# A hybrid encoder step on one core: weight splits started one phase earlier, and attention scores as three rounded products

## What is computed

```python
xn = rmsnorm(x, norm1_w)
proj = xn @ w_in                      # z | x,B,C | dt | q | k | v
y_ssm = ssm_group(...)                # conv, chunked scan, gate, norm
o_sb  = stick_breaking(q, k, v, ...)  # z = q.k * 64**-0.5 ; suffix sums of log-sigmoid ; w @ v
h = x + concat(y_ssm, o_sb) @ w_out
...
def peer_rows(xr, wq, k1, k2, u_tab, v_tab):
    q = xr @ wq
    ...                               # top 16 per half, then top 16 of the sums
    act  = gelu(u_tab[expert] @ xr)
    coef = softmax(best) * act
    return sum(coef * v_tab[expert])
out = rmsnorm(h + peer(rmsnorm(h, norm2_w)))
```

## Time and profile before

| | us |
|---|---|
| median of 3 runs (3828.84 to 3840.70) | 3835.93 |
| the profiled execution | 3835.56 |
| its span in the profile | 3833.8 |
| PE busy in it | 3375.1 |
| DVE busy in it | 2605.1 |
| POOL busy in it | 1772.6 |
| ACT busy in it | 1103.4 |

### The profile page before, as it was taken

The page is one execution under the profiler, slowest core; times in us unless marked ns, Lnnn a source line. Parts: engine busy times, 40 slices in busy tenths (PEclk is TensorE's granted clock), DMA queues, the critical chain, the costliest instruction groups (busy, mean ns, idle before and its releaser), DMA issues. The chain is left out here.

```text
span 3833.8 us, 47422 instructions
## 1 busy us (share of the span) xinstructions
PE 3375.1 (88%) x16719; PEld 2866.7 (75%) x16719; DVE 2605.1 (68%) x4637; ACT 1103.4 (29%) x2170; POOL 1772.6 (46%) x1282
## 2 busy tenths in 40 slices
PE   5998799596899989999998689895999997888998
PEld 4998644333478989999998688884887775667776
DVE  3412644264536888999996466665887786988995
ACT  2322243232322211111111222222443333433343
POOL 1000143666300000688887578885888884333320
PEclk9999787686899999999999799997999998999999
DMA  2123099999611125555554699998999998999995
GB/s 78 49 78 126 18 419 371 324 316 324 215 68 60 38 70 170 170 178 167 175 174 130 236 333 354 346 344 304 353 363 345 347 345 310 407 388 400 401 386 181
DMA packets 281863, 945.35 MB, mean 247 GB/s; under 512 B 54432, under 2 KB 155936, under 8 KB 218688
## 3 DMA queue, kind: packets, MB, share of 16 engines
q1 hardware_dynamic: 209280, 583.52, 43.5%
q0 software_dynamic: 70656, 352.78, 24.1%
q10 hardware_dynamic: 1728, 6.49, 0.4%
HBM read 742.76 MB, written 199.45 MB: 246 GB/s over the span
## 5 line engine op out<-in xcount | busy, mean ns | idle before, releaser
L1579 POOL DMA_INDIRECT scratch_gates<-routes_merged,routes_at x768 | 1020.9, 1329 | 631.6 <-DVE routes_merged L1811 363.9
L2037 PE MATMUL val_acc<-n_hi 128*128 128x512 f32 x1536 | 617.3, 402 | 135.0 <-DVE n_lo L2072 132.1
L2038 PE MATMUL val_acc<-n_lo,n_hi 128*128 128x512 f32 x1536 | 609.5, 397 | 0.0
L2039 PE MATMUL val_acc<-n_hi,n_lo 128*128 128x512 f32 x1536 | 608.7, 396 | 0.0
L1626 POOL DMA_INDIRECT sparse_rows<-in_uv_rows,routes_at x256 | 382.4, 1494 | 379.3 <-DVE mixed L1660 322.1
L1637 DVE CUSTOM_DVE_ANT_0 sparse_rows<-sparse_rows,mixed 128x1024 f32<-128x1024 f32 x288 | 350.6, 1220 | 208.4 <-DMA sparse_rows<-in_uv_rows,routes_at 187.2
L2037 PEld LDWEIGHTS val_acc<-n_hi 128*128 128x128 f32 x1536 | 295.1, 192 | 225.5 <-DVE n_lo L2061 147.8
L123 PE MATMUL route_hidden<-n_hi,route_u_both 128*128 128x384 f32 x1280 | 432.5, 338 | 11.5 <-DMA route_u_both<-scratch_u_split 11.5
L124 PE MATMUL route_hidden<-n_lo,route_u_both 128*128 128x384 f32 x1280 | 434.3, 339 | 0.0
L125 PE MATMUL route_hidden<-n_hi,route_u_both 128*128 128x384 f32 x1280 | 432.8, 338 | 0.0
L1660 DVE SCALAR_TENSOR_TENSOR mixed<-sparse_rows,sparse_coef,mixed 128x1024 f32<-128x1024 f32 x288 | 363.7, 1280 | 9.4 <-ACT sparse_coef L1651 9.1
(11 more groups left out here) (288 smaller groups left out, 6225.1 us busy)
## 6 DMA issues: line engine op xcount, KB each, us to landing
val_v_raw<-in_v_rows SPq DMA_DIRECT2D x256, 512.0 KB, 6.9
scratch_u_split<-sb_u_both SPq DMA_DIRECT2D x80, 1024.0 KB, 5.1
route_u_both<-scratch_u_split SPq DMA_DIRECT2D x80, 1024.0 KB, 5.6
scratch_gates<-gate POOLq DMA_DIRECT2D x32, 1536.0 KB, 80.2
val_gate<-scratch_gates SPq DMA_DIRECT2D x256, 192.0 KB, 7.4
val_coef<-scratch_hidden SPq DMA_DIRECT2D x256, 192.0 KB, 7.8
conv<-in_peer_u SPq DMA_DIRECT2D x80, 512.0 KB, 6.0
scratch_hidden<-route_hidden_out SPq DMA_DIRECT2D x160, 192.0 KB
```

Of the source, the lines that this page charges most:

```text
L1579: pool.indirect_dma_start(self.t["gates"].rearrange("c r (l o) -> (c r l) o", o=1), bass.IndirectOffsetOnAxis(ap=self.routes.at[:, i, slot ...
L2037: nc.tensor.matmul(out, c_hi[:, s, tok], v_hi[:, s, to], start=(j == 0), stop=False)
L2038: nc.tensor.matmul(out, c_hi[:, s, tok], v_lo[:, s, to], start=False, stop=False)
L2039: last = nc.tensor.matmul(out, c_lo[:, s, tok], v_hi[:, s, to], start=False, stop=(j == KEYS - 1))
```

## The change

- 54 of the 80 ahead-of-time splits move from attention to the input projection. There POOL itself issues the loads and the stores, in the order load j+1, split j, store j; the landing place is part of `mixed`, which the first norm no longer needs. SP waits for the last stores ahead of the tails of the convolution. Attention keeps 26 splits, in buffers of its own.
- Attention's prompt scores become three products of fp32r parts with 64 rows. ACT writes `q_hi` (with the scale, in place of the scaling of q) and `k_hi`, DVE `q_lo` and `k_lo`, once for each pair.
- The inputs of pairs 2 and 3 are loaded behind the 26 splits, each as soon as its buffer is free.
- `conv` and `gate` are freed ahead of attention, which makes room for the new buffers.
- 320 scatters instead of 350 are issued in routing, and 460 instead of 500 by the end of the hidden phase, so 308 instead of 268 in the first value pass.

```diff
-SCATTER_FROM, ROUTE_SCATTERS = 17, 350
-HIDDEN_SCATTERS = 500
+SCATTER_FROM, ROUTE_SCATTERS = 17, 320
+HIDDEN_SCATTERS = 460
-PAIR_LOADS = {30: 2, 57: 3}
+FIRST_SPLITS = 54
...
+        presplit = Presplit(nc, t, sb, sem, raw, 0, FIRST_SPLITS)
...
                 with sp.Fori(1, pairs) as i:
                     load(i)
+                presplit.end(sp)
                 sp.wait_ge(convolved, STEPS * (CONV_TILES + 2))
...
                 nc.gpsimd.memset(result[:, :, :TAPS - 1], 0.0).then_inc(cleared, 1)
+                presplit.load(pool, 0)
+                for j in range(FIRST_SPLITS):
+                    if j + 1 < FIRST_SPLITS:
+                        presplit.load(pool, j + 1)
+                    presplit.split(pool, j)
+                    presplit.store(pool, j)
...
-                for j in range(EARLY_ROUTE):
-                    if j + 1 < EARLY_ROUTE:
+                for j in range(presplit.tiles):
+                    if j + 1 < presplit.tiles:
                         presplit.load(sp, j + 1)
                     presplit.store(sp, j)
-                    if j in PAIR_LOADS:
-                        p = PAIR_LOADS[j]
-                        sp.wait_ge(pv_done, 4 + JN * (p - 1))
-                        inputs.load(sp, p, p % 2)
+                for p in range(2, PAIRS):
+                    sp.wait_ge(pv_done, 4 + JN * (p - 1))
+                    inputs.load(sp, p, p % 2)
                 presplit.end(sp)
...
-                    nc.scalar.activation(q[:, u, :PROMPT], q[:, u, :PROMPT], ACT.Copy, scale=HD ** -0.5).then_inc(scaled, 1)
+                    nc.scalar.activation(q_hi[:, u], q[:, u, :PROMPT], ACT.Copy, scale=HD ** -0.5).then_inc(scaled, 1)
+                    nc.scalar.activation(k_hi[:, u], k[:, u, :PROMPT], ACT.Copy).then_inc(scaled, 1)
...
-                        last = nc.tensor.matmul(z[:, job.slot, job.cols], k[hp, u, job.j * P:job.j * P + P],
-                                                q[hp, u, job.qb * QW + job.lo:job.qb * QW + QW],
-                                                start=True, stop=True, skip_group_check=True)
+                        out = z[:, job.slot, job.cols]
+                        nc.tensor.matmul(out, k_hi[hp, u, keys], q_hi[hp, u, queries], start=True, stop=False, skip_group_check=True)
+                        nc.tensor.matmul(out, k_hi[hp, u, keys], q_lo[hp, u, queries], start=False, stop=False, skip_group_check=True)
+                        last = nc.tensor.matmul(out, k_lo[hp, u, keys], q_hi[hp, u, queries], start=False, stop=True, skip_group_check=True)
...
-                    pe.wait_ge(scaled, 3 * p + 3)
+                    pe.wait_ge(scaled, 4 * p + 4)
+                    pe.wait_ge(low_ready, 2 * p + 2)
...
+                    dve.wait_ge(scaled, 4 * p + 3)
+                    nc.vector.scalar_tensor_tensor(q_lo[:, u], q[:, u, :PROMPT], HD ** -0.5, q_hi[:, u].bitcast(F32),
+                                                   ALU.mult, ALU.subtract).then_inc(low_ready, 1)
+                    dve.wait_ge(scaled, 4 * p + 4)
+                    nc.vector.tensor_tensor(k_lo[:, u], k[:, u, :PROMPT], k_hi[:, u].bitcast(F32), ALU.subtract).then_inc(low_ready, 1)
```

More of the change, by code:

```diff
@@ L247, in spread, with input_projection @@
     return last
-def input_projection(nc, consts, x_hi, x_lo, dt_raw, conv_wb, conv, gate, t):
+def input_projection(nc, consts, x_hi, x_lo, dt_raw, conv_wb, conv, gate, t, raw):
     STEPS = TAPS + 1
@@ L806, in load, with attention_phase @@
                      t["past_v"][bass.ds(p, 1)].rearrange("a p b d -> (a p) (b d)")).then_inc(landed, 16)
-def attention_phase(nc, consts, t, inputs, mixed, zeros, raw, zeroed):
+def attention_phase(nc, consts, t, inputs, mixed, zeroed):
     jobs = attention_jobs()
@@ L825, in attention_phase @@
         strict, strict_masked, neg_ones = sb("strict", [P, P]), sb("strict_masked", [P, P]), sb("neg_ones", [P, P])
+        q_hi, q_lo = sb("q_hi", [P, 2, PROMPT], F32R), sb("q_lo", [P, 2, PROMPT], F32R)
+        k_hi, k_lo = sb("k_hi", [P, 2, PROMPT], F32R), sb("k_lo", [P, 2, PROMPT], F32R)
+        low_ready = sem("low_ready")
         z = ps("z", [P, 4, QW])
@@ L835, in attention_phase @@
             sem("sums_ready"), sem("w_ready"), sem("pv_done"), sem("o_copied"), sem("dve_step"), sem("passed"))
-        presplit = Presplit(nc, t, sb, sem, raw)
+        zeros = sb("zeros", [P, ZERO_COLS])
+        presplit = Presplit(nc, t, sb, sem, sb("u_raw", [P, 2, DC, P]), FIRST_SPLITS, EARLY_ROUTE - FIRST_SPLITS)
         def keys_of(job):
@@ L861, in _ @@
                 nc.gpsimd.memset(q_diag[:], 0.0).then_inc(cleared, 1)
-                nc.gpsimd.memset(zeros, 0.0).then_inc(zeros_cleared, 1)
+                nc.gpsimd.memset(zeros[:], 0.0).then_inc(zeros_cleared, 1)
                 pool.wait_ge(zeros_cleared, 1)
@@ L865, in _ @@
                 for a in range(ZERO_DMAS):
-                    pool.dma_start(gates[a], zeros).then_inc(zeroed, 16)
-                for j in range(EARLY_ROUTE):
+                    pool.dma_start(gates[a], zeros[:]).then_inc(zeroed, 16)
+                for j in range(presplit.tiles):
                     presplit.split(pool, j)
@@ L1070, in soft, with pair @@
                     dve.wait_ge(sp_ready, JN * p + job.n + 1)
-                def pair(p):
+                def pair(p, u):
                     links = []
+                    dve.wait_ge(scaled, 4 * p + 3)
[3 more added lines that the diff above has]
+                    nc.vector.tensor_tensor(k_lo[:, u], k[:, u, :PROMPT], k_hi[:, u].bitcast(F32), ALU.subtract).then_inc(low_ready, 1)
                     clip(p, jobs[0])
@@ L1082, in _ @@
                     for u in range(2):
-                        pair(2 * i + u)
+                        pair(2 * i + u, u)
 def mix_phase(nc, consts, mixed, m_hi, m_lo, w2_row, t):
@@ L1507, with __init__ @@
 class Presplit:
-    def __init__(self, nc, t, sb, sem, raw):
-        self.nc, self.t, self.raw = nc, t, raw
+    def __init__(self, nc, t, sb, sem, raw, base, tiles):
+        self.nc, self.t, self.raw, self.base, self.tiles = nc, t, raw, base, tiles
         self.both = sb("u_both", [P, 2, 2, DC, P], F32R)
@@ L1520, in load @@
             sp.wait_ge(self.low, j - 1)
-        sp.dma_start(self.raw[:, j % 2], self.t["peer_u"][j + EARLY_RETRIEVE]).then_inc(self.landed[j % 2], 16)
+        sp.dma_start(self.raw[:, j % 2], self.t["peer_u"][j + self.base + EARLY_RETRIEVE]).then_inc(self.landed[j % 2], 16)
     def store(self, sp, j):
         sp.wait_ge(self.low, j + 1)
-        sp.dma_start(self.t["u_split"][j], self.both[:, j % 2].bitcast(F32)).then_inc(self.stored[j % 2], 16)
+        sp.dma_start(self.t["u_split"][j + self.base], self.both[:, j % 2].bitcast(F32)).then_inc(self.stored[j % 2], 16)
     def end(self, sp):
         for u in range(2):
-            sp.wait_ge(self.stored[u], 16 * ((EARLY_ROUTE + 1 - u) // 2))
+            sp.wait_ge(self.stored[u], 16 * ((self.tiles + 1 - u) // 2))
     def split(self, pool, j):
@@ L2130, in build @@
         with ExitStack() as inner:
-            conv = inner.enter_context(nc.sbuf_tensor("conv", [P, CONV_TILES, CONV_OUT], F32))
-            gate = inner.enter_context(nc.sbuf_tensor("gate", [P, Z_TILES, TOK], F32))
+            window = inner.enter_context(ExitStack())
+            conv = window.enter_context(nc.sbuf_tensor("conv", [P, CONV_TILES, CONV_OUT], F32, side="right"))
+            gate = window.enter_context(nc.sbuf_tensor("gate", [P, Z_TILES, TOK], F32, side="right"))
             with ExitStack() as early:
@@ L2136, in build @@
                 norm_phase(nc, "norm1", mixed, norm1_w, consts, hi=x_hi, lo=x_lo, src_dram=t["x"])
-                input_projection(nc, consts, x_hi, x_lo, dt_raw, conv_wb, conv, gate, t)
+                raw = mixed[:].rearrange("p k t -> p (k t)")[:, :2 * D].rearrange("p (s k m) -> p s k m", s=2, m=P)
+                input_projection(nc, consts, x_hi, x_lo, dt_raw, conv_wb, conv, gate, t, raw)
             inputs = AttentionInputs(nc, t, inner)
@@ L2144, in build @@
             ssd_phase(nc, consts, (ssm_norm_w, d_skip), head_vec, dt_raw, conv, gate, t, mixed, prefetch)
-            zeros = gate[:].rearrange("p z t -> p (z t)")[:, :ZERO_COLS]
-            raw = conv[:].rearrange("p c t -> p (c t)")[:, :2 * D].rearrange("p (s k m) -> p s k m", s=2, m=P)
-            attention_phase(nc, consts, t, inputs, mixed, zeros, raw, zeroed)
+            window.close()
+            attention_phase(nc, consts, t, inputs, mixed, zeroed)
         with nc.Block() as block:
```

1 line of the change is left out of this document (added).

## The result

The change takes 3789.53 us against 3834.76 for the kernel before (medians of four runs each): a ratio of 0.9872, 95% interval 0.9834 to 0.9909. Forecast were 3806, faster, and 3772 to 3842. The time fell by 45 us, where the sum said 30. Single runs of the changed kernel lie between 3770 and 3793, so a few us between two medians of it mean nothing.

A forecast was written before the change was run, and what follows sets the result against it. The prediction took PE to bound the input projection, PE and late pair loads attention, and POOL's queue routing through the first value pass. Terms 20 - 55 + 5 = -30 on 3835.56 gave 3806 us, range 3772 to 3842.

The forecast's parts named there:

- Input projection: Input projection: the 54 splits on POOL end the stage near 370, 20 us behind the old end; bounds 0 and 50.
- what DVE runs between two of POOL's instructions is added to POOL's time: Input projection: POOL and DVE take turns on SBUF operands, adding 43 us to POOL's end, 327 becoming 370.
- My 4.9: Input projection: POOL's time for a split tile in us, taken from SP's two-deep loop, set by the landing of loads.
- The rule of the Trainium skill that I had put aside: Input projection: loads issued by POOL land 0.4 us later than SP's, making the sum 11 us higher; left out.
- Attention's waits: Attention: earlier loads let pair 2 start 26 us earlier and remove the 24.7 us wait ahead of pair 3.
- the clock's rival: Attention: PE idles more, the mean clock falls from 0.75 to 0.66, costing 64 us, result 3870; chance 0.07.
- The three products: Attention, pairs 2 and 3: rounded score products save 8 us; extra ACT and DVE operations cost 4 back.
- The scatters: Routing, hidden and first value pass: moving scatters costs 5 us more net, since POOL is full on both sides.
- Covered splits: Input projection: PE still sets the end, POOL ends before 350, result 3786; chance 0.17.
- The starved convolution: Input projection: DVE's convolution waits for POOL and delays PE's weight splits, 64 us, result 3850; chance 0.13.
- Scatters that do not weigh: First value pass: bound by transfers, not POOL, so 40 more scatters cost nothing, result 3750; chance 0.03.

The follow-up runs named there:

- the idle splits: The change, with POOL repeating a split's two operations 54 times behind its 26 splits in attention, without transfers: 3831.63 us, ratio to before 0.9990.
- both edits: The change with pair 2's inputs loaded behind store 14 and three landing places for the input projection's expert tiles: 3749.43 us; with float32 scores 3763.98.
- the run with three landing places: The change with three landing places instead of two for the input projection's expert tiles, loads issued two tiles ahead: 3763.43 us, ratio to before 0.9826.

## Why the prediction was right, and what it had wrong

**Direction and range were right**, and the sum was 15 us short. It is nearer than its terms, since the input projection came out 12 worse and attention 28 better. By its terms:

*Input projection, +20 forecast, +32 measured.* That POOL would end the stage was right; the stage ends at 382.6 where the forecast had 370. The 12 us between them are what is left of two larger errors of opposite sign, so the nearness is luck. The step "what DVE runs between two of POOL's instructions is added to POOL's time", priced at 43, measured 12.5 to 16 in POOL's instructions: in the turns it is DVE that loses, 58 us of busy time, and PE's end moves by only 4. In return a tile took 5.86 us from store to store. A tile that meets neither a turn nor a wait takes 4.92, of which 0.30 is idle time ahead of the store's issue that I had left out (16 us in all). My 4.9, from SP's loop, was meant to hold the waits for loads; here they come on top, 42 us. The two errors are not wholly apart: a tile takes 6.3 us while DVE convolves (the first 20) and 5.3 behind PE's end, so some of the waits for loads may follow from the turns. The rule of the Trainium skill that I had put aside (DMA: Bandwidth & Descriptors, Latency and other measured facts) pointed that way: loads issued by POOL land in 6.7 us (median), those by SP landed in 6.0. The two ran in different traffic, so this doesn't prove the issue path. The last 10.3 us, from the issue of the last store through the tails to the next stage, were forecast as 8.3.

*Attention's waits, -26 and -24.7 forecast.* Right in mechanism and size: pair 2 starts 29 us sooner in the phase, still waiting for its load, and the wait ahead of pair 3 is gone. The wait ahead of pair 2 was 19.5 us where I said around 10, since pairs 0 and 1 ended 14 us sooner. (Pair 2 took 119.1 us before and not the 117 that I read from the earlier trace rows; that enters only the price of the clock's rival.)

*The three products, -8 and +4 for pairs 2 and 3; measured -29.* **This is the step that failed, by what it left out.** I priced the turns of POOL and DVE in the stage that receives the splits, and not in the one that they leave. There they had made pairs 2 and 3 some 15 us longer each; with POOL gone that came back, with float32 scores too, and POOL without transfers takes it away again. Only 9 of the 29 us are PE's idle time; 20 are its busy time, at a higher granted clock (with float32 scores 21: 204.7 us for 225.8). That POOL's work alone can lower the clock is shown (0.86 to 0.72 in pair 2, with the idle splits); how much of the 20 comes that way isn't. The price of a product was about right. A job of 512 columns at the full clock, in pair 2 of the change:

```profile
802.23 0.50 PE L957 MATMUL sb_z<-sb_q_hi,sb_k_hi 64*128 64x512 f32 x1
802.57 0.39 PE L958 MATMUL sb_z<-sb_q_lo,sb_k_hi 64*128 64x512 f32 x1
802.80 0.39 PE L959 MATMUL sb_z<-sb_q_hi,sb_k_lo 64*128 64x512 f32 x1
```

That is 0.96 us from 802.23 to 803.19, for 0.86 forecast and 1.12 of the float32 product. What it is worth in time lies between nothing (the run with float32 scores beside the change) and 3.6 us a pair (with both edits); 2 net was taken.

*The scatters, +5 forecast.* Routing, hidden and the value phase to the last scatter changed by -31.8, -15.1 and +44.5, which is -2; the value phase behind the last scatter is 6 longer, in a part that nothing touches. Putting the numbers back changed no time. Right: the work was moved.

*The rivals.* Covered splits: no, POOL ends 23 us behind PE. The starved convolution: its mechanism is there (a tile's DVE work grew, PE ended 4 us later) and turns into a price as soon as POOL is denser. The clock did not fall in attention, where the rival had it; there it rose from 0.75 to 0.81. It fell from 0.99 to 0.95 in the input projection, whose last 33 us have no product of PE. Scatters that do not weigh: no.

## What to carry to other kernels

Work that is moved off a shared resource has two ends: price the stage that it leaves with the same rule as the stage that receives it. On POOL, subtractions and casts on SBUF operands cost DVE time even where no semaphore joins the two, so "POOL is free here" is to be read with DVE's rows beside it: which of its operations have SBUF operands, and who waits for them. And a queue that pauses may be the reason why its neighbour runs: before a loop is made denser, look whether the pauses are somebody's turns. Beside the early load of pair 2, moving less (49 in place of 54, 3743 and 3741 us) gave at least as much as making POOL faster (3749).

## What was not expected of the hardware

- The price is not in proportion to how much POOL does. In pair 2, 82 us of POOL's work with pauses for loads had made the pair some 15 us longer; 140 us without pauses made it 41 longer; in pair 3, 42 us without pauses at the pair's start made it 5 longer. How much of that is density and how much the place in the pair is not separated. The copy of 128 x 128 on DVE took 227, 557 and 1380 ns with POOL absent, pausing and dense; the operation that reads PE's accumulators took 691 or 692 in all three.
- DVE loses more than POOL in the turns: 58 us of busy time against 12.5 to 16 in the input projection. A copy of three columns for each partition (L397) took 1479 ns there, and 162 before.
- Without any edit, pairs of equal work took 104.6 and 110.4 us in one profile and 110.4 and 104.7 in the next, each time with a mean granted clock of 0.86 in the shorter and 0.81 in the longer: a pair's time on its own tells nothing under some 6 us. The sum of two was 215 in both, but 211 in the run with three landing places, whose attention is the same code, so it tells nothing under some 4.
